# Third mixer of a fused three-layer kernel: another order of its S5 recurrences, latent tiles and attention

## The reference, cut to what matters

```python
def odd_mixer(h, pos, w_in, lam_re, lam_im, log_step, b_re, b_im, c_re, c_im, d_skip, w_glu, b_glu,
              q_norm, w_uq, kv_norm, w_ukv, w_out):
    u, c_q, c_kv, k_rope = split_cols(h @ w_in, ODD_SIZES)          # 512, 384, 256, 32 columns
    y_c = s5_group(u, lam_re, lam_im, log_step, b_re, b_im, c_re, c_im, d_skip, w_glu, b_glu)
    y_d = mla_group(c_q, c_kv, k_rope, pos, q_norm, w_uq, kv_norm, w_ukv)
    return jnp.concatenate([y_c, y_d], axis=-1) @ w_out

def s5_group(u, ...):            # 32 groups of 16 channels, 64 complex states each
    bu = einsum(ug, b_bar)       # inputs of the states
    state = associative_scan(s5_combine, (a_bar, bu), axis=1)       # over the 512 tokens
    y = real(einsum(state, cm)) + d_skip * ug
    y = gelu(y)
    return y * sigmoid(y @ w_glu + b_glu)

def mla_group(c_q, c_kv, k_rope, pos, q_norm, w_uq, kv_norm, w_ukv):
    q = rms_norm(c_q, q_norm) @ w_uq          # 8 heads of 64 plain and 32 rotated
    kv = rms_norm(c_kv, kv_norm) @ w_ukv      # 8 heads: 64 for keys, 64 for values
    ...                                       # rope, chunk-causal softmax, values
```

## Time and profile before

| | |
|---|---|
| median of 3 runs | 2554.46 us (2553.76 to 2554.94) |
| the profiled execution | 2556.53 us |
| its span, first to last instruction | 2554.7 us |
| PE busy | 2469.6 us, 97% |
| DVE, ACT, POOL busy | 51%, 34%, 42% |
| chain that ended last | PE 86%, DVE 10%, ACT 2%, issue 2%, DMA 0% |
| mean granted clock of TensorE | 0.985 |

### The profile page before, as it was taken

How to read it: one execution, slowest core, us unless ns; L and a number is a source line. 1 busy time by engine, 2 the same in 40 slices (tenths; PEclk the granted TensorE clock), 3 DMA queues, 4 the chain that set the end, 5 groups by cost and what they waited for, 6 DMA issues and landing times.

```text
span 2554.7 us, 30093 instructions
## 1 busy us (share of the span) xinstructions
PE 2469.6 (97%) x11694; PEld 1976.1 (77%) x11694; DVE 1296.2 (51%) x1928; ACT 868.2 (34%) x1360; POOL 1061.4 (42%) x830
## 2 busy tenths in 40 slices
PE   8999999999999999999989999999999889999998
PEld 6877667888888888876767778888888756788886
DVE  6336687533633321585757655586126865533301
ACT  4453246222322222244444433322224353322221
POOL 4323244654544445353222245455453222544442
PEclk9999999999999999999999999999998999999999
DMA  4212122322332333221111123332331112222232
GB/s 147 69 56 77 62 72 87 99 93 89 111 96 94 99 94 96 95 79 58 50 50 50 50 74 106 99 99 90 97 98 51 31 34 64 98 99 92 95 98 78
DMA packets 62573, 209.44 MB, mean 82 GB/s; under 512 B 6880, under 2 KB 9184, under 8 KB 62304
## 3 DMA queue, kind: packets, MB, share of 16 engines
q1 hardware_dynamic: 61424, 204.11, 25.0%
q10 hardware_dynamic: 1008, 3.41, 0.4%
HBM read 205.39 MB, written 2.10 MB: 81 GB/s over the span
## 4 chain that ended last, share of the span: by engine, by line
PE 86%; DVE 10%; ACT 2%; issue 2%; DMA 0%; DVEq 0%; ACTq 0%; SPq 0%
PE ps L617 24%; PE ps L619 24%; PE ps L618 24%; DVE T L2163 1%; PE ps L638 1%; PE ps L639 1%; PE ps L640 1%; PE ps L958 1%; PE ps L734 1%; ACT A L1600 1%; PE ps L725 1%; PE ps L991 1%; PE ps L978 1%; PE ps L812 1%; DVE small L2310 1%
## 5 line engine op out<-in xcount | busy, mean ns | idle before, releaser
L588 POOL TENSOR_TENSOR w_lo<-w_raw,w_hi 128x512 fp32r<-128x512 f32 (+4 forms) x822 | 1051.6, 1303 | 1454.9 <-ACT w_hi L1296 1454.7
L617 PE MATMUL ps<-H,w_hi 128*128 128x512 f32 x1880 | 756.5, 402 | 22.6 <-DVEq L1858 11.7
L619 PE MATMUL ps<-H,w_lo 128*128 128x512 f32 x1880 | 738.0, 393 | 0.0
L618 PE MATMUL ps<-H,w_hi 128*128 128x512 f32 x1880 | 737.2, 392 | 0.0
L1296 ACT CAST w_hi<-w_raw 128x1024 fp32r<-128x1024 f32 (+4 forms) x411 | 402.9, 984 | 523.7 <-DMA w_raw<-in_weights_dram 517.4
L617 PEld LDWEIGHTS ps<-H,w_hi 128*128 128x128 f32 x1880 | 356.1, 189 | 115.6 <-issue 24.4
L617 PE MATMUL ps<-split,w_hi 128*128 128x512 f32 x1034 | 411.5, 398 | 6.8 <-issue 3.3
L619 PEld LDWEIGHTS ps<-H,w_lo 128*128 128x128 f32 x1880 | 355.7, 189 | 75.8
L618 PEld LDWEIGHTS ps<-H,w_hi 128*128 128x128 f32 x1880 | 356.3, 190 | 73.2 <-issue 2.6
L619 PE MATMUL ps<-split,w_lo 128*128 128x512 f32 x1034 | 403.7, 390 | 0.0
L618 PE MATMUL ps<-split,w_hi 128*128 128x512 f32 x1034 | 403.5, 390 | 0.0
(11 more groups left out here) (405 smaller groups left out, 2401.1 us busy)
## 6 DMA issues: line engine op xcount, KB each, us to landing
w_raw<-in_weights_dram SPq DMA_DIRECT2D x323, 512.0 KB, 3.5
w_raw<-in_weights_dram SPq DMA_DIRECT2D x48, 448.0 KB, 3.2
w_raw<-in_weights_dram SPq DMA_DIRECT2D x22, 256.0 KB, 2.6
X<-in_xt_dram SPq DMA_DIRECT2D x4, 512.0 KB, 7.8
out_dram<-A SPq DMA_DIRECT2D x8, 256.0 KB, 2.1
w_raw<-in_weights_dram SPq DMA_DIRECT2D x12, 128.0 KB, 2.0
w_raw<-in_weights_dram SPq DMA_DIRECT2D x6, 192.0 KB, 2.3
A<-in_w_gates_dram ACTq DMA_DIRECT2D x1, 1024.0 KB, 4.9
```

Source lines behind the costliest of these rows:

```text
L588: sub = nc.gpsimd.tensor_tensor(w_lo[:, p % NS, c], w_raw[:, p % NS, c], w_hi[:, p % NS, c].bitcast(F32), ALU.subtract)
L617: mm_(ps[:, bank, :], r(wh), xh, start=(k == 0), stop=False)
L618: mm_(ps[:, bank, :], r(wh), xl, start=False, stop=False)
L619: mm = mm_(ps[:, bank, :], r(wl), xh, start=False, stop=(k == kt - 1))
```

## The change

The columns of od_in are reordered: tiles 0 to 2 query latents as before, then S5 inputs 0 to 2 (tiles 3 to 5), the key and value latents (6 and 7), the last S5 input (8) and the rotated key (9). Recurrences 0, 1 and 2 get work buffers outside the area that holds h, so they don't wait until od_in has been read; the buffers of 0 to 2 are partly the same ones, and the states of each have their own place. The tables of recurrences 0 and 1 are made beside the tiles of down2. The spread of BB and the cast of the positions go from VectorE to ScalarE. The eight turns are mixed into od_in 4. Then each engine's order is written anew, and all four outputs_of, regroup and halve come ahead of the attention's first transposes; the attention's fill starts with glu. Cut to its core:

```diff
@@ ORDER
-    + tiles_of("od_in") + tiles_of("uq") + tiles_of("uk", 0, 1) + tiles_of("uv", 0, 1) + tiles_of("uk", 1)
-    + tiles_of("uv", 1) + tiles_of("glu")
+    + tiles_of("od_in") + tiles_of("uq") + tiles_of("uk", 0, 2) + tiles_of("uv", 0, 1)
+    + tiles_of("glu", 0, 3) + tiles_of("uk", 2, 3) + tiles_of("glu", 3) + tiles_of("uk", 3) + tiles_of("uv", 1)
@@ buffers
-        od_slot = lambda t: t + 4 if t < 6 else t - 6
+        od_slot = (4, 5, 6, 0, 1, 2, 7, 8, 3, 9)
+        U_TILE = (3, 4, 5, 8)
+        U_BANK = (7, 7, 4, 6)
-        S5X = [h_tile(6), h_tile(7)]
-        S5G = [h_tile(8), h_tile(9)]
-        S5H = [[h_tile(10 + 2 * i), h_tile(11 + 2 * i)] for i in range(2)]
-        S5T = [h_tile(14), h_tile(15)]
+        S5X = [SG, SG, [area(27312, S), area(27824, S)], [h_tile(6), h_tile(7)]]
+        S5G = [[area(24240, S), area(24752, S)]] * 3 + [[h_tile(8), h_tile(9)]]
+        S5H = [[area(26288, S), area(26800, S)], SG, [area(27312, S), area(27824, S)],
+               [h_tile(12), h_tile(13)]]
+        S5T = [area(25264, S)] * 3 + [h_tile(14)]
@@ fill of the attention
-        MLA_FILL = (3, 3, 2, 2, 5, 6, 5, 0, 4, 4, 4, 4, 4, 4, 4, 4)
+        FILL_MLA = ([(tile, 4) for tile in tiles_of("glu", 0, 3)] + [(("uk", 2), 2), (("glu", 3), 4), (("uk", 3), 2), (("uv", 1), 4)]
+                    + [(tile, 4) for tile in tiles_of("out3a")])
+        MLA_FILL = (0,) + (4,) * 12 + (3, 3, 2)
@@ tensor engine: waits, and the order
             def regroup_in(m):
-                pe.wait_ge(s_od, 7 + m)
+                pe.wait_ge(s_od, U_TILE[m] + 1)
...
             def inputs_of(s):
+                if s == 0:
+                    pe.wait_ge(s_direct, 1)
+                if s == 1:
+                    pe.wait_ge(s_rt, COLS["cq"] + 1)
+                if s == 2:
+                    pe.wait_ge(s_rr, NORM["cq"] + 1)
+                if s == 3:
+                    pe.wait_ge(s_rr, NORM["ckv"] + 1)
                 pe.wait_ge(s_gs, s + 1)
...
+            for i, _ in enumerate(zip(units(("od_in", 4), HX), turns_b())):
+                if i == 5:
+                    regroup_in(0)
             pe.wait_ge(s_s5w, 8)
             inputs_of(0)
+            norm_cols("cq")
+            now = units(("od_in", 5), HX)
+            run(now, 1)
+            regroup_in(1)
+            run(now, 2)
+            inputs_of(1)
+            run(now, 2)
+            pe.wait_ge(s_buf, 1)
+            norm_spread("cq", 5)
+            run(now, 8)
+            tile("od_in", 6, HX)
             regroup_in(2)
+            tile("od_in", 7, HX)
+            inputs_of(2)
+            now = units(("od_in", 8), HX)
+            run(now, 4)
+            pe.wait_ge(s_buf, 2)
+            norm_cols("ckv", 7)
+            run(now, 8)
+            now = units(("od_in", 9), HX)
+            run(now, 3)
+            regroup_in(3)
+            norm_spread("ckv")
+            run(now, 8)
             pe.wait_ge(s_mq, 3)
             tile("uq", 0, QC)
+            inputs_of(3)
             rotate_mla(0)
             tile("uq", 1, QC)
             pe.wait_ge(s_s5c, 2)
             outputs_of(0)
+            rotate_mla(1)
+            tile("uq", 2, QC)
+            rotate_mla(2)
+            tile("uq", 3, QC)
+            outputs_of(1)
+            tile("uq", 4, QC)
+            regroup(0)
+            tile("uq", 5, QC)
+            outputs_of(2)
+            regroup(1)
             pe.wait_ge(s_mq, 5)
             tile("uk", 0, KC)
+            tile("uk", 1, KC)
+            pe.wait_ge(s_roped, 16 + 3)
+            mla_scores(0)
+            outputs_of(3)
             for _ in token_units(("uv", 0), KC):
                 pass
+            regroup(2)
+            regroup(3)
@@ scalar engine
+            def first_tables(t):
+                if t == 1:
+                    act.wait_ge(s_s5p, 2)
+                    turns(0)
+                    turns(1)
+                if t == 3:
+                    sines(0)
+                    sines(1)
...
+            for i in range(6):
+                copy_b(i)
+            copy_in(0)
+            copy_b(6)
+            copy_b(7)
             root("cq")
             hi_to(last_panel("od_in", 5) + 4)
+            copy_in(1)
             act.wait_ge(s_ang, 2)
             link(A_(SINM, ANGM, ACT.Sin))
             A_(COSM, ANGM, ACT.Sin, scale=0.5).then_inc(s_sin, 1)
+            hi_to(last_panel("od_in", 6) + 4)
+            square_od("ckv", 0, 6)
+            act.wait_ge(s_h2, 1)
+            sines(2)
+            copy_in(2)
+            hi_to(last_panel("od_in", 7) + 4)
+            square_od("ckv", 1, 7)
             hi_to(last_panel("od_in", 8) + 4)
+            act.wait_ge(s_h2, 2)
+            sines(3)
+            hi_to(last_panel("od_in") + 4)
+            root("ckv", 7)
+            copy_in(3)
...
+            gelu(3)
+            values(0)
+            hi_to(last_panel("uv", 0) + 5)
+            halve(2)
             nc.scalar.preload_act_table_set("exp_and_others")
+            halve(3)
@@ vector engine
+            first, second, third, fourth = [recurrence_parts(s) for s in range(4)]
             run(first, 1)
+            od(5)
+            run(first, 1)
+            copy_rms("cq", RQ, 5)
+            run(first, 1)
+            run(second, 1)
+            od(6)
+            run(second, 2)
+            latents(QC, 0, OD[:, 4, :], vec("od_q_norm", 0), RQ)
+            od(7)
+            run(third, 1)
+            add_square("ckv", 1)
+            run(third, 1)
+            od(8)
+            run(third, 1)
+            rms("ckv")
+            for k in (1, 2):
+                latents(QC, k, OD[:, 4 + k, :], vec("od_q_norm", k), RQ)
+            dve.wait_ge(s_sin, 2)
+            cosine(COSM)
             od(9)
+            copy_rms("ckv", RK)
             rope_mla(0)
+            run(fourth, 1)
             rope_mla(1)
+            run(fourth, 1)
             rope_mla(2)
+            run(fourth, 1)
+            for k in range(2):
+                latents(KC, k, OD[:, 7 + k, :], vec("od_kv_norm", k), RK)
+            split_gelu(0)
             mla_maxima(0)
+            for m in range(1, 4):
+                split_gelu(m)
             mla_maxima(1)
```

More of the change, by code:

```diff
@@ L1235, in fill_mla @@
             def fill_mla():
-                for t in (1, 2, 3):
-                    yield from units(("uk", t), KC)
+                pe.wait_ge(s_yg, 4)
+                for t in range(3):
+                    yield from units(("glu", t), YG)
+                yield from units(("uk", 2), KC)
+                yield from units(("glu", 3), YG)
+                yield from units(("uk", 3), KC)
                 yield from token_units(("uv", 1), KC)
-                pe.wait_ge(s_yg, 4)
-                for t in range(4):
-                    yield from units(("glu", t), YG)
                 pe.wait_ge(s_yc, 4)
@@ L1251, in _ @@
                 run(fill, n // 2)
-                if s == 1:
-                    outputs_of(3)
-                if s == 2:
-                    regroup(3)
                 pe.wait_ge(s_pn, 32 + s + 1)
@@ L1473, in _, with ffn @@
             x_squares("out1", "ffn1")
-            def ffn(k, after, beside=None):
+            def ffn(k, after, beside=None, beside_down=None):
                 norm = f"ffn{k}"
@@ L1665, in sines, with turns @@
                 A_(cs, cs, ACT.Identity, scale=-2.0, bias=con("ones")[:, 0:1]).then_inc(s_tabx, 1)
+            def turns(s):
+                for t in range(4 * s, 4 * s + 4):
+                    turn = A_(TURNS[s][:, CH * (t % 4):CH * (t % 4) + CH], lvec("time", 0, CH), ACT.Copy,
+                              scale=s5[:, 2, t:t + 1])
+                turn.then_inc(s_turn, 1)
+            def first_tables(t):
[6 more added lines that the diff above has]
+                    sines(1)
+            ffn(2, "mix3", s5_scales, first_tables)
+            act.dma_start(POSM.bitcast(I32), positions.to_broadcast([P, S])).then_inc(s_pos, 16)
             def col(name):
                 return lvec(name, 0, 256).rearrange("p (t c) -> p t c", t=16)
-            act.wait_ge(s_s5p, 2)
+            act.wait_ge(s_s5z, 1)
+            for half in range(2):
+                rows = slice(64 * half, 64 * half + 64)
+                for c in range(2):
+                    spread = nc.scalar.copy(BW[rows, c].rearrange("p t (j h n) -> p t j h n", j=TAPS, h=2)[:, :, :, half, :],
+                                            BB[rows, c])
+            spread.then_inc(s_s5b, 1)
             hi_to(last_panel("od_in", 0) + 4)
@@ L2120, in _, with ffn @@
             add_to_x("out1", "ffn1", lambda k: ("norm_ffn", k))
-            def ffn(k, after, gain, beside=None):
+            def ffn(k, after, gain, beside=None, beside_down=None):
                 norm = f"ffn{k}"
@@ L2457, in latents @@
                 dve.sem_inc(s_mq, 1)
-            dve.wait_ge(s_s5z, 1)
-            for half in range(2):
-                rows = slice(64 * half, 64 * half + 64)
-                for c in range(2):
```

(11 more changed lines are left out.)

256 lines of the change are left out of this document (79 added, 177 removed).

## The result

| | before | changed |
|---|---|---|
| median | 2550.74 us (2543.11 to 2556.97, 19 runs) | 2557.26 us (2549.46 to 2567.53, 19 runs) |
| ratio to before | | 1.0028, 95% interval 1.0016 to 1.0040 |
| the profiled execution | 2556.53 us, span 2554.7 | 2556.39 us, span 2554.6 |
| PE busy | 2469.6 us, 97% | 2463.3 us, 96% |
| chain that ended last: PE, VectorE | 86%, 10% | 85%, 11% |

The change costs 7.1 us (4.1 to 10.2). A second group of runs gave 1.0022 (1.0008 to 1.0036), 5.6 us. The forecast was 4.7 us slower, just under the 5.1 that the prediction took as the least that a measurement can tell. As a time, 2559.2 was forecast and 2557.26 measured. That this is only 1.9 off is in part luck: the three runs of the kernel before that the forecast started from have a median of 2554.46, the 19 runs here 2550.74.

What follows compares the result with a forecast made beforehand. TensorE, busy 97%, bounds the kernel, so only its waits and clock move the end. 2046.6 + 17.5 + 84.6 = 2148.7, with clock falls 8.5 and POOL 1.0 2158.2, 4.7 later: 2559.2 us, range 2547 to 2568.

Steps and rivals of the forecast that it cites:

- The waits forecast: PE in the third mixer: new waits of 5.6 at inputs_of(2) and 7.7 at norm_cols(ckv), smaller ones behind; 18.8 becomes 26.
- the sign of being right: inputs_of(2) late by copy_in, norm_cols(ckv) by add_square, together over 10 us; first transposes 13 to 20 us later than 2048.
- the prediction's central step: Up to the second key latent, VectorE runs late from 1973.4; the clock fall behind PE's 5.6 wait is free.
- clock falls, POOL: Added to the full-clock sum: 8.5 us for clock falls on the path, 1.0 for VectorE slowed beside POOL.
- the first leg: From 1949.04, where od_in 3 ends, to the second key latent at 2046.6; VectorE's work 69.9 and waits 3.3 from 1973.4.
- The second and third leg: Second key latent to first transposes, 17.5; then the attention to the end of mla_values(3), 84.6 where it took 105.2.
- the three falls: PE's clock falls on the path behind the waits of 7.7, 2.2 and 2.5, at 2.8 each, 8.5 us in all.
- The tail: What follows mla_values(3), that is out3b, feed-forward and norm: untouched by the change.
- Ahead of T: Ahead of 1949: copies moved from VectorE to ScalarE and tables made in down2 cost nothing.
- Rival (b): od_in 3 with tap products, at 0.57 before: new order ahead keeps 2.4 GHz, up to 10.2 us less, 2549; chance 0.11.
- Rival (a): PE's clock stays up behind the shorter waits, nothing lost: 4 to 7 us earlier, 2549; chance 0.15.
- (c): Clock falls twice more on the path, as in od_in 4 or first attention steps: +5.6, POOL's full 3, 2567; chance 0.19.

Runs made afterwards that it cites:

- e1: Changed kernel with ScalarE's copy_in(2) ahead of square_od of the first key latent and sines(2): 2561.66 us, 1.0032 to the kernel before.
- e3: Changed kernel with two VectorE operations left out of the turning and two of the turning back in each recurrence (states differ): 2550.25 us, 0.9992 to before.
- e8: Kernel with all reorderings and new second-leg order, plus tap products mixed into od_in 2 and 3, two behind each unit: 2538.30 us, 0.9950 to before.
- e10: Changed kernel with only the tap products mixed into od_in 2 and od_in 3, two behind each unit: 2554.60 us, 1.0009 to before.
- e2: Changed kernel with VectorE running the first recurrence whole, scans and states too, ahead of od(5): 2553.32 us, 1.0011 to before.
- e4: Changed kernel with PE taking the whole of od_in 8, not half, ahead of norm_cols(ckv): 2555.32 us, 1.0010 to before.
- e7: Changed kernel with all reorderings, plus scores(1) ahead of regroup(3), exponential table and first exponentials ahead of value copies, step 0 scaled earlier: 2543.47 us, 0.9974 to before.
- e9: Kernel before with od_in 3 whole and all 32 tap products in one block behind it: 2550.07 us, 0.9998 to before.

## Why the prediction came out so

*The mechanism was right, in its order and nearly in its sizes.* The waits forecast were 5.6, 7.7, 1.9, 0.7, then 1.8, 2.2 and 2.5; the trace has 5.5, 6.7, 1.5, 0.5, then 2.8, 2.0 and 2.5, each at the line and behind the releaser named. The first two make 12.2 us, where over 10 was given as the sign of being right, and the first transposes come 16.5 us later than 2048, where 13 to 20 was. That the first is free and VectorE carries was the prediction's central step, and e1 (no gain) and e3 (one for one) show it.

*The sum, leg by leg*, from T and against the second profile, which drew the same clock as the profile of before:

| us | forecast, full clock | measured |
|---|---|---|
| T to the second key latent | 99.7 | 108.4 |
| to the first transposes | 17.5 | 19.0 |
| to the end of mla_values(3) | 84.6 | 87.3 |
| clock falls, POOL | 8.5 + 1.0 | in the rows above |
| sum | 211.3 | 214.7 |

The forecast is 3.4 short: 4.9 in the first leg, less 1.4 that was too much behind it. The second and third leg are 4.2 over their full-clock values, and two of the three falls at 2.8 had been set aside for them. They came behind the 2.8 and the 2.5, not behind the 2.2, and last 3.4 us each at 0.50, so they cost 1.7 each; the one behind norm_cols(ckv) goes on for 7.2 us and costs 3.6. The third fall and the 1.0 leave 103.5 for the first leg. The other 4.9 are three terms, each too small. (1) VectorE's waits for PE were set at 0.8 for od_in 8 and 2.5 for the rotation; they are 4.2 and 3.1, so 4.0 more. Of these the fall's 2.8 is already counted, since od_in 8 is late by PE's half clock behind its wait; 1.2 remain. (2) VectorE's work from od(5) on is 80.1 less 7.3 of waits, 72.8, where 69.9 plus 1.0 was forecast: 1.9. The slowed operations in it come to 2.8 over their usual times. They lie where GpSimd works; the one of 1.12 stands beside this:

```profile
2037.47 2.11 POOL L592 TENSOR_TENSOR w_lo<-w_raw,w_hi 128x256 fp32r<-128x256 f32 x2 [3.96 <-ACT w_hi L1309]
```

(3) od(5) came 28.3 after T, not 26.5. That is the remaining 1.7, and here errors cancel. The forecast starts at 1949.04, "where od_in 3 ends". The trace of the kernel before has od_in 3 and its products ended at 1946.9, with the first turn behind them:

```profile
1946.87 1.09 PE L1083 MATMUL ps<-C_,A 128*128 128x128 f32 x4
```

By 1949.04 this turn and the first unit of od_in 4 had run, and the sum counts both again, 1.1 at the full clock. Against this the steps up to od(5), 24.3 by the forecast, took 25.6 in the first profile, at the full clock: 1.3 more. And the low clock of the tap stretch lasts into od_in 4 for longer than before (to 1951.5 in the second profile): od(5) comes 2.7 later after T there than at the full clock, and the start at 1949.04 had taken in only some 1.0 of that. So the 1.7 is the clock's; the 1.1 and the 1.3 nearly cancel, by luck.

*The tail* was costed at nothing. It is 401.2 in both profiles of before, 402.4 and 402.2 in those of the changed kernel, and up to 404.6 in variants. That is 1.0 more, and it goes with the clock: in the tail PE is at 0.50 for 11.5 us in both profiles of before, for 13.7 and 13.9 in those of the changed kernel, and for 19.8 in e1, e8 and e10, where the tail is 404.3 to 404.5. No step of the change stands there, and two profiles each don't show whether the change has a part in it.

*Ahead of T* the forecast was no cost for the moved copies and tables. The heads agree to 0.2 at the low clock. The tables made beside down2 lie ahead of the head; the mixer's first matmul comes at 1906.4 before and at 1905.2 in the second profile of the changed kernel, with 20.5 us at 0.50 ahead of it in both, so no cost shows there either. Right.

*Rival (b)* was right that the tap stretch can run at the full clock, at 8.5 us rather than 10.2, but wrong about its reason: with the same instructions and the same order it comes out either way. So one profile at the full clock is a draw and no gain of the change. Whether the change alters the odds stays open: two of two profiles of the kernel before fell there and four of nine of the changed one and its variants, and the mean granted clock, 0.987 for both kernels, is one of the whole span and can't tell. With the same odds for both, the change would cost the 8.0 by which these two spans differ; the medians say 7.1 and 5.6. *Rival (a)*, the clock stays up behind the waits, did not occur, but for the wait of 2.0 at regroup(3), which no fall follows directly; *(c)* in part: GpSimd's share came to 2.9, near its full 3, and the low clock reached into od_in 4, but no two further falls lie on the path.

*What the forecast left open* is which side of 0.2% the 4.7 would fall. Its own 4.7, the 3.4 missing up to V and the 1.0 of the tail make 9.1 of a span comparison, less 1.2 since this execution reached the mixer earlier: 8.0, as the spans say. The medians say 7.1 and 5.6.

## What to carry to other kernels

When work is pulled ahead of an attention, ask which engine makes it, not which engine uses it: PE's order moved, but the recurrences are VectorE's, and every wait of PE was a symptom of one queue. Such a leg is shortened by filling the carrying engine's own gaps (e2, e4: about 3.5 us of leg each) and by taking slow items of a third engine from ahead of the first thing that is needed (e7: 5.6 us), not by removing a long wait that the profile shows on PE (e1: 5.5 us removed, nothing gained). And compare two profiles only after looking whether both drew the same clock in the stretches whose instructions are the same.

## What the runs showed of the hardware

TensorE's clock can fall without any wait ahead of it. In od_in 3, where four tap products of 32 columns stand behind each three matmuls of 512, PE is busy throughout and fell to 0.50 for over 20 us in 4 of 9 profiles of one and the same sequence, and stayed at 1.00 in 5. With two of them behind each unit it stayed up in both profiles taken (e8, e10), and all of them in a block let it fall in the block, in the one profile taken (e9). Two profiles alone could be chance at five in nine; that the mean granted clock of the runs rose as well (0.991 for 0.988 to 0.989, and 0.989 for 0.987) speaks for the mix. The Trainium skill (TensorE: Matmul & The Clock Gate, HAM oscillation) tells of falls behind idle gaps. This case's traces differ: between 1850 and 1940 us they have no wait of PE, and the clock of 0.55 over a fully busy 23.7 us shows that a gap is not needed.

This one stretch is worth 8.5 us of 2550, more than the change under study, where executions of one kernel spread over some 16 us. It is not the only one: ahead of the third mixer PE is at 0.50 for 10.2 to 30.7 us, depending on the execution, which makes up to 10 us more.

VectorE's operations can be held up by GpSimd's: beside its tensor_tensor, 128x512 elementwise operations took 0.96 to 1.12 us where 0.69 is usual, and in e2 two scans of 128x128 took 1.43 and 1.34 where 0.40 and 0.42 are usual.
